# Feed-forward stages with eight pairs instead of six, each followed by half of a four-chunk down product

## The chip, the cores and the metric

The kernel runs on one core of one Trainium2 chip. The metric is the device time of one execution in microseconds (us). Engines are named as the profile names them: PE (TensorE, matmul), DVE (VectorE), ACT (ScalarE), POOL (GpSimd), SP (SyncE, which issues the DMAs).

## The reference, cut to what matters

512 positions of width 1024 go through two blocks. Each has mixers that this change leaves alone, and there are three gated feed-forward stages: one in the first block, two in the second.

```python
def rms_norm(x, g, eps=NORM_EPS):
    x32 = x.astype(jnp.float32)
    y = x32 * lax.rsqrt(jnp.mean(x32 * x32, axis=-1, keepdims=True) + eps)
    return (y * g.astype(jnp.float32)).astype(x.dtype)

# first block, D_FF = 2816
h = rms_norm(x, norm_ffn_pre_g[l])
f = (jax.nn.silu(h @ w_gate[l]) * (h @ w_up[l])) @ w_down[l]
x = x + rms_norm(f, norm_ffn_post_g[l])

# second block, twice
def swiglu(h, w_gu, w_down):
    gu = h @ w_gu
    gate, up = jnp.split(gu, 2, axis=-1)
    return (jax.nn.silu(gate) * up) @ w_down
x = x + 0.5 * swiglu(rmsnorm(x, ffn1_norm[l]), ffn1_w_gu[l], ffn1_w_down[l])
```

All is float32.

## The kernel before

**Storage.** Activations lie transposed: 128 features on the partitions, 512 positions along the free axis, so a width of 1024 is 8 chunks. Each float32 operand is split in two rounded parts, high (`HH`, `GH`, `WH`) and low (`HL`, `GL`, `WL`), and every product is three matmuls: high by high, low weight by high, high weight by low (lines 1328, 1330, 1332). An output tile of 128 features from 8 chunks is 24 matmuls of 512 columns; one from 4 chunks is 12.

**Weights.** Each weight tile is loaded whole by SP into one of four slots `RAW` (line 2432). ACT then makes the high part (`split`, line 1573) and DVE the low part (line 1864). The parts live in a ring of six halves; a weight tile takes two halves whatever its number of chunks, a weight of a pair (below) takes one. ACT may write a half only when PE has finished the weight that held it, and SP may fill a raw slot only when DVE has made the low part of what lay there (`raw_done`).

**Pairs.** A feed-forward stage has 22 output tiles for the gate and 22 for up. Two tiles that stand side by side can be made together, as a *pair*: `pair` replaces 2x2x2 block products of half size by seven (`MIXED`, Winograd's form). One side of a pair (gate or up) is 7 products of 4 chunks x 3 matmuls = 84 matmuls of 256 columns (`product`, lines 1356, 1358, 1360), where two plain tiles are 48 of 512. Four of the seven weights are sums of weight blocks, which POOL makes from two raw slots (`combine_weights`, line 2311, sums 1 to 4). The products are added up by DVE (lines 1890, 1900, 1903, 1908, 1917, 1926), ACT applies silu, and POOL multiplies gate by up for three quarters of the pair (`gate_mixed`, line 2333: one of 128x512, one of 128x256; the "gate products"). Then `split_tile` (ACT line 1667, DVE line 1982) writes the two tiles of the pair into `GH` and `GL`, where the down product reads them. The seventh product adds onto a bank that DVE's line 1903 must have read.

**A stage** (`ffn`, called once per stage) works in thirds, `THIRDS`: 6, 8 and 8 tiles. The first six tiles are plain (`PLAIN`), since the mixed inputs are only being made then. In each other third, pairs stand at tiles 0, 3 and 6 (`PAIRS`) and a plain tile at 2 and 5. After each third the down product over that third's 6 or 8 chunks follows, 8 output tiles `mt`, and DVE adds each to `X` or to the stage's output tiles (lines 2098, 2080, 2083). During the first down product, `place` (ACT line 1583, DVE line 1883) writes the normalized input over `HH` and `HL`, one chunk per output tile. The last third of the last stage is done by `last_down`, whose last 4 chunks run in two halves of positions.

**Order.** There is no scheduler on the chip. A `Plan` lists steps; each engine runs its own steps strictly in that order and waits by semaphores. `ahead` and `split_to` put the split of a weight where its ring halves are certain to come free. `split_to` also puts the sums of a coming pair: after each split it looks at the next 8 weights (`LOOK`) and emits sums whose raws have been asked for, as long as fewer than 2 whole (not pair) weights stand in between.

## Time and profile before

| | us |
|---|---|
| runs | 1922.88, 1921.64, 1922.81 |
| median | 1922.81 |
| the profiled execution | 1921.05 |
| its span | 1919.3 |

The span is what the profile's rows cover; 1.75 us lie around it. The profile's page gives busy times by engine and by fortieths of the span, and the trace gives every instruction with its start, its duration and the idle time ahead of it. A matmul's duration overlaps the next one's, so what one costs is read from the distance between starts. Busy shares: PE 99%, DVE 64%, ACT 44%, POOL 26%.

### The profile page before, as it was taken

How to read it: one execution, taken by the hardware profiler on the slowest of the kernel's cores; microseconds unless marked ns; L12 is line 12 of the kernel's file. 1: busy time of each engine (PE TensorE's matmuls, PEld its weight loads, DVE VectorE, ACT ScalarE, POOL GpSimd, SP SyncE). 2: the span in 40 equal slices, each digit the busy share in tenths (PEclk: the TensorE clock that was granted, in tenths of full speed). 3: DMA queues.
4: the chain of work that ended last, by engine and by line, in shares of the span. 5: the costliest groups of instructions: out<-in, count | busy, mean ns of one | idle time of the engine just before them, and what ended most of it. 6: DMA issues, size and time to landing. Idle time of an engine off the chain costs nothing.

```text
span 1919.3 us, 27787 instructions
## 1 busy us (share of the span) xinstructions
PE 1895.8 (99%) x10930; PEld 1602.8 (84%) x10930; DVE 1231.6 (64%) x1869; ACT 852.3 (44%) x1453; POOL 498.7 (26%) x422
## 2 busy tenths in 40 slices
PE   9999999999999999999999999999899999999998
PEld 7777788878998998789989888777777788998997
DVE  6677535476775674767657657887754456775665
ACT  6344524454443443544424446665543344442444
POOL 5101001214352431225323432222010023442330
PEclk9999999999999999999999999999999999999999
DMA  6222133332433343333434332222332233333332
GB/s 175 60 66 67 55 105 101 114 99 83 116 89 110 88 120 100 88 88 88 114 87 119 100 99 67 67 67 67 88 99 57 76 88 91 108 89 110 89 104 83
DMA packets 340787, 176.56 MB, mean 92 GB/s; under 512 B 6481, under 2 KB 339378, under 8 KB 340658
## 3 DMA queue, kind: packets, MB, share of 16 engines
q1 hardware_dynamic: 340658, 174.79, 31.6%
q8 instruction: 87, 1.43, 0.3%
q14 instruction: 42, 0.34, 0.1%
HBM read 172.67 MB, written 2.10 MB: 91 GB/s over the span
## 4 chain that ended last, share of the span: by engine, by line
PE 84%; DVE 7%; issue 3%; ACT 3%; POOL 2%; DMA 1%; ACTq 0%; SPq 0%; POOLq 0%; DVEq 0%
PE ps L1328 21%; PE ps L1332 20%; PE ps L1330 20%; PE ps L1356 5%; PE ps L1360 5%; PE ps L1358 5%; DVE WL L1864 2%; PE ps L1422 1%; POOL TS L2311 1%; DMA RAW<-in_ffn_w_gu 1%; POOL TS L2333 1%; DVE GL L1982 1%; PE ps L1402 1%; PE ps L1411 1%; PE ps L1507 1%
## 5 line engine op out<-in xcount | busy, mean ns | idle before, releaser
L1864 DVE TENSOR_TENSOR WL<-RAW,WH 128x1024 fp32r<-128x1024 f32 (+2 forms) x371 | 408.6, 1107 | 221.1 <-ACT WH L1573 217.7
L1573 ACT ACTIVATE WH<-RAW 128x1024 fp32r<-128x1024 f32 (+2 forms) x371 | 326.2, 886 | 312.7 <-PE ps L1332 264.6
L1328 PE MATMUL ps<-HH,WH 128*128 128x512 f32 x1152 | 461.4, 400 | 1.0 <-ACT HH L1620 1.0
L1332 PE MATMUL ps<-HL,WH 128*128 128x512 f32 x1152 | 449.7, 390 | 0.8 <-DVE HL L1946 0.8
L1330 PE MATMUL ps<-HH,WL 128*128 128x512 f32 x1152 | 449.1, 390 | 0.4 <-DVE WL L1864 0.4
L1328 PE MATMUL ps<-GH,WH 128*128 128x512 f32 x688 | 269.4, 392 | 0.0
L1332 PE MATMUL ps<-GL,WH 128*128 128x512 f32 x688 | 268.1, 390 | 0.0
L1330 PE MATMUL ps<-GH,WL 128*128 128x512 f32 x688 | 267.9, 389 | 0.0
L1328 PEld LDWEIGHTS ps<-HH,WH 128*128 128x128 f32 x1152 | 216.3, 188 | 53.5 <-issue 8.2
L1332 PEld LDWEIGHTS ps<-HL,WH 128*128 128x128 f32 x1152 | 216.2, 188 | 49.1 <-DVE HL L1946 2.1
L1330 PEld LDWEIGHTS ps<-HH,WL 128*128 128x128 f32 x1152 | 216.5, 188 | 47.7 <-issue 4.1
L2311 POOL TENSOR_TENSOR TS<-RAW 128x512 f32<-128x512 f32 x72 | 102.3, 1421 | 352.4 <-issue 259.8
L1360 PE MATMUL ps<-NL,WH 128*128 128x256 f32 x576 | 163.0, 283 | 0.0
L1358 PE MATMUL ps<-NH,WL 128*128 128x256 f32 x576 | 163.0, 283 | 0.0
L1356 PE MATMUL ps<-NH,WH 128*128 128x256 f32 x576 | 162.9, 283 | 0.0
L1864 DVE TENSOR_TENSOR WL<-TS,WH 128x512 fp32r<-128x512 f32 x144 | 132.0, 927 | 42.0 <-ACT WH L1573 40.5
L1332 PEld LDWEIGHTS ps<-GL,WH 128*128 128x128 f32 x688 | 129.1, 188 | 28.1 <-DVE GL L1982 1.3
L1328 PEld LDWEIGHTS ps<-GH,WH 128*128 128x128 f32 x688 | 129.2, 188 | 27.8 <-ACT GH L1667 0.8
L1330 PEld LDWEIGHTS ps<-GH,WL 128*128 128x128 f32 x688 | 129.2, 188 | 27.0 <-issue 0.5
L2342 POOL TENSOR_TENSOR TS<-TS 128x512 f32<-128x512 f32 (+1 forms) x42 | 53.0, 1261 | 297.0 <-ACT TS L1631 294.6
L1356 PE MATMUL ps<-HH,WH 128*128 128x256 f32 x432 | 123.2, 285 | 3.0 <-DVE TS L1903 2.8
L1358 PE MATMUL ps<-HH,WL 128*128 128x256 f32 x432 | 122.2, 283 | 0.0
(251 smaller groups left out, 3048.6 us busy)
## 6 DMA issues: line engine op xcount, KB each, us to landing
RAW<-in_ffn_w_gu SPq DMA_DIRECT2D x88, 512.0 KB, 3.8
RAW<-in_w_in SPq DMA_DIRECT2D x67, 512.0 KB, 3.7
RAW<-in_ffn_w_down SPq DMA_DIRECT2D x24, 512.0 KB, 3.8
RAW<-in_w_gate SPq DMA_DIRECT2D x22, 512.0 KB, 3.9
RAW<-in_w_up SPq DMA_DIRECT2D x22, 512.0 KB, 3.8
RAW<-in_w_out SPq DMA_DIRECT2D x16, 512.0 KB, 3.7
RAW<-in_mem_w_kv SPq DMA_DIRECT2D x16, 512.0 KB, 3.8
RAW<-in_w_down SPq DMA_DIRECT2D x16, 512.0 KB, 3.8
```

The lines of the kernel that those rows point to most:

```text
L1328: e.matmul(bk, wh, xh, start=k == 0, stop=False)
L1330: e.matmul(bk, wl, xh, start=False, stop=False)
L1332: last = e.matmul(bk, wh, xl, start=False, stop=k == kt - 1)
L1356: e.matmul(bk, wh[:, c, :], xh, start=i < 5 and c == 0, stop=False, skip_group_check=i >= 5)
L1358: e.matmul(bk, wl[:, c, :], xh, start=False, stop=False, skip_group_check=i >= 5)
L1360: o = e.matmul(bk, wh[:, c, :], xl, start=False, stop=c == 3, skip_group_check=i >= 5)
L1402: e.matmul(at.bank(("sc", (u, half), i))[:, 0:n], at.tile(q[0])[s, i * P:(i + 1) * P], at.tile(k[0])[s, 0:n], start=True, stop=True).then_ ...
L1411: o = e.transpose(bk[:, c:c + P], m["L"][half][:, lo[i] + j * P:lo[i] + (j + 1) * P], ident)
L1573: e.activation(at.weight(n, "H"), at.raw(n), ACT.Copy).then_inc(*sg.inc("hi", n))
L1864: e.tensor_tensor(at.weight(n, "L"), at.raw(n), at.weight(n, "H").bitcast(F32), ALU.subtract).then_inc(*sg.inc("lo", n))
L2311: e.tensor_tensor(out, x, y, op).then_inc(*sg.inc("comb", (key, j)))
L2342: e.tensor_tensor(a, a, s, ALU.add).then_inc(*sg.inc("acc", (acc, c)))
```

## The change

`THIRDS` and `PAIRS` go. A stage now has six plain tiles, then `SEGMENTS`: pieces of the down product over 4 chunks (`"down", n, first chunk, chunks, first mt, last mt`) and pairs by turns. Eight pairs cover tiles 6 to 21. Each four-chunk down product is cut in two halves, one ahead of a pair and one behind it: 5 and 3 output tiles for the first, 4 and 4 for the other three. What remains, `REST`, is the down product over chunks 16 to 21, after the last pair. So each output tile is added up in five parts and not three. `place` handles two chunks per output tile in the first four. The split tiles of a pair are emitted behind the second and third output tile of the down piece that follows. `last_down` keeps its 4 chunks in halves of positions and has 2 chunks ahead of them in place of 4. `split_to` emits sums while fewer than 3 whole weights stand in between.

```diff
-THIRDS = ((0, 6), (6, 8), (14, 8))
-PAIRS = ((), (0, 3, 6), (0, 3, 6))
+SEGMENTS = (("down", 0, 0, 4, 0, 5), ("pair", 6), ("down", 0, 0, 4, 5, KD), ("pair", 8),
+            ("down", 1, 4, 4, 0, 4), ("pair", 10), ("down", 1, 4, 4, 4, KD), ("pair", 12),
+            ("down", 2, 8, 4, 0, 4), ("pair", 14), ("down", 2, 8, 4, 4, KD), ("pair", 16),
+            ("down", 3, 12, 4, 0, 4), ("pair", 18), ("down", 3, 12, 4, 4, KD), ("pair", 20))
+REST = (16, 6)
+LAST = 4
...
-                if w[0] == "sum" and need < self.n_dma and whole < 2:
+                if w[0] == "sum" and need < self.n_dma and whole < 3:
                     self.combine_to(w[1], max(w[2], self.combined.get(w[1], 0)))
...
+        for kind, n, *rest in SEGMENTS:
+            if kind == "pair":
+                G, f = third0 + n // 8, n % 8
+                self.pair(gen, G, f, 0, gate, g0 + n * P, pending)
+                done = self.pair(gen, G, f, 1, up, u0 + n * P, pending)
...
+            for mt in range(m0, m1):
+                b = self.bank(("db", third0, f0, mt))
+                if n == 0 and mt < 4:
+                    self.place(gen, next(unplaced), plain)
+                    self.place(gen, next(unplaced), plain)
+                mm, = self.mtiles([(down, f0, nf, mt * P)], ("G", third0 + f0 // 8, f0 % 8), [b], ahead=False)
+                evac(n, mt, b, mm)
+                if mt > m0 and pending:
+                    self.split_tile(*pending.pop(0))
+                self.ahead(len(self.weights))
...
+        for first, cnt in GROUPS:
+            mts = range(first, first + cnt)
+            banks = [self.bank(("db", third0, f0, mt)) for mt in mts]
+            mms = self.mtiles([(down, f0, nf, mt * P) for mt in mts], ("G", third0 + f0 // 8, f0 % 8), banks, ahead=False)
...
-            mm, = self.mtiles([(down, f0, nf - 4, mt * P)], ("G", G, 0), [b])
+            mm, = self.mtiles([(down, f0, 2, mt * P)], ("G", G, 0), [b])
```

**POOL around the end of a pair.** L2311 are the sums for the next pair, L2333 the gate products of the pair that ends; the semaphores `s_d_raw` tell that a raw slot has landed. Before, with a plain tile between the pairs:

```order
104 L2311 TENSOR_TENSOR TS<-RAW 128x512 [waits s_xl,s_d_raw3,s_d_raw2]
105 L2311 TENSOR_TENSOR TS<-TS,RAW 128x512 [waits s_lo,s_comb]
106 L2311 TENSOR_TENSOR TS<-RAW 128x512 [waits s_lo]
107 L2311 TENSOR_TENSOR TS<-RAW,TS 128x512 [waits s_lo,s_comb]
108 L2333 TENSOR_TENSOR TS<-TS 128x512 [waits s_gate_act,s_part_sum]
109 L2311 TENSOR_TENSOR TS<-RAW 128x512 [waits s_lo,s_d_raw1,s_d_raw0]
110 L2311 TENSOR_TENSOR TS<-TS,RAW 128x512 [waits s_lo,s_comb]
111 L2333 TENSOR_TENSOR TS<-TS 128x256 [waits s_gate_act,s_part_sum]
```

After, with four down tiles between the pairs:

```order
94 L2333 TENSOR_TENSOR TS<-TS 128x512 [waits s_gate_act,s_part_sum]
95 L2311 TENSOR_TENSOR TS<-RAW 128x512 [waits s_xl,s_d_raw1,s_d_raw0]
96 L2311 TENSOR_TENSOR TS<-TS,RAW 128x512 [waits s_lo,s_comb]
97 L2311 TENSOR_TENSOR TS<-RAW 128x512 [waits s_lo]
98 L2333 TENSOR_TENSOR TS<-TS 128x256 [waits s_gate_act,s_part_sum]
99 L2311 TENSOR_TENSOR TS<-RAW,TS 128x512 [waits s_comb]
100 L2311 TENSOR_TENSOR TS<-RAW 128x512 [waits s_lo,s_d_raw3,s_d_raw2]
101 L2311 TENSOR_TENSOR TS<-TS,RAW 128x512 [waits s_lo,s_comb]
```

The second gate product stands behind the first three sums of the next pair, as it stood behind six sums before.

**DVE between two pairs.** L1917 and L1926 are a pair's last additions, L1864 the low parts of weights (from `TS`: of a sum; from `RAW`: of a whole tile or a half), L1982 the split tiles, L2073 the plain tile's product, L2083 the addition of a down tile. Before:

```order
568 L1917 TENSOR_TENSOR TS<-ps,TS 128x256 [waits s_mm]
569 L1864 TENSOR_TENSOR WL<-TS,WH 128x512 [waits s_hi]
570 L1926 TENSOR_TENSOR TS<-ps,TS 128x256 [waits s_mm]
571 L1864 TENSOR_TENSOR WL<-TS,WH 128x512 [waits s_hi]
572 L1864 TENSOR_TENSOR WL<-RAW,WH 128x512 [waits s_hi]
573 L1864 TENSOR_TENSOR WL<-TS,WH 128x512 [waits s_hi]
574 L1982 TENSOR_TENSOR GL<-TS,GH 128x512 [waits s_part_sum,s_gm,s_xh]
575 L1982 TENSOR_TENSOR GL<-TS,GH 128x512 [waits s_xh]
576 L1864 TENSOR_TENSOR WL<-RAW,WH 128x512 [waits s_hi] x2
577 L2073 TENSOR_TENSOR TS<-ps,TS 128x512 [waits s_gate_act,s_mm]
```

After:

```order
591 L2083 TENSOR_TENSOR TS<-ps,TS 128x512 [waits s_dn,s_mm]
592 L1864 TENSOR_TENSOR WL<-RAW,WH 128x512 [waits s_hi]
593 L2083 TENSOR_TENSOR TS<-ps,TS 128x512 [waits s_dn,s_mm]
594 L1982 TENSOR_TENSOR GL<-TS,GH 128x512 [waits s_part_sum,s_gm,s_xh]
595 L1864 TENSOR_TENSOR WL<-TS,WH 128x512 [waits s_hi] x2
596 L2083 TENSOR_TENSOR TS<-ps,TS 128x512 [waits s_dn,s_mm]
597 L1982 TENSOR_TENSOR GL<-TS,GH 128x512 [waits s_xh]
598 L1864 TENSOR_TENSOR WL<-RAW,WH 128x512 [waits s_hi]
599 L1864 TENSOR_TENSOR WL<-TS,WH 128x512 [waits s_hi]
600 L2083 TENSOR_TENSOR TS<-ps,TS 128x512 [waits s_dn,s_mm]
601 L1864 TENSOR_TENSOR WL<-RAW,WH 128x512 [waits s_hi] x2
```

Before, the first four weights of the next pair (569 to 573) stood ahead of the first split tile; after, the first two (595) stand behind it.

## Rows read from the trace of the kernel before

**Rows 1.** The page: busy time of PE, and its busy and clock slices.

```profile
PE 1895.8 (99%) x10930; PEld 1602.8 (84%) x10930; DVE 1231.6 (64%) x1869; ACT 852.3 (44%) x1453; POOL 498.7 (26%) x422
...
PE   9999999999999999999999999999899999999998
...
PEclk9999999999999999999999999999999999999999
```

**Rows 2.** Windows of stage one (stretch, length, busy by engine, clock, DMA): pair, plain tile, down.

```profile
504.73:524.88 20.15, 20.15 (x169) 20.15 (x168) 14.43 (x24) 9.76 (x17) 3.38 (x3) 1.00 0.46 130
524.88:535.79 10.91, 10.91 (x51) 9.02 (x49) 6.08 (x7) 3.57 (x7) 10.83 (x9) 1.00 0.17 50
...
713.81:757.35 43.54, 43.54 (x194) 36.04 (x193) 19.12 (x20) 13.29 (x17) 8.49 (x7) 1.00 0.34 99
```

**Rows 3.** Timeline of PE (start, duration in us): first matmul of a pair, plain tile, next pair.

```profile
504.73 0.28 PE L1356 MATMUL ps<-NH,WH 128*128 128x256 f32 x1
...
524.88 0.40 PE L1328 MATMUL ps<-HH,WH 128*128 128x512 f32 x1
...
535.79 0.28 PE L1356 MATMUL ps<-NH,WH 128*128 128x256 f32 x1
```

**Rows 4.** PE's waits in pairs: groups by form (busy, mean ns, idle before), and timeline.

```profile
L1356 PE MATMUL ps<-HH,WH 128*128 128x256 f32 x432 | 123.2, 285 | 3.0 <-DVE TS L1903 2.8
...
576.11 0.39 PE L1356 MATMUL ps<-HH,WH 128*128 128x256 f32 x1 [0.47 <-DVE TS L1903]
```

**Rows 5.** SP: timeline of raw loads in the first pair, and the page's time to landing.

```profile
515.32 2.40 SPq L2432 DMA_DIRECT2D RAW<-in_w_gate  x2
...
RAW<-in_w_gate SPq DMA_DIRECT2D x22, 512.0 KB, 3.9
```

**Rows 6.** Timeline of POOL: first pair's end, plain tile; after the third pair.

```profile
522.15 1.30 POOL L2311 TENSOR_TENSOR TS<-RAW 128x512 f32<-128x512 f32 x1 [16.69 <-DVE WL L1864]
523.53 2.22 POOL L2311 TENSOR_TENSOR TS<-TS,RAW 128x512 f32<-128x512 f32 x1
525.71 1.29 POOL L2311 TENSOR_TENSOR TS<-RAW 128x512 f32<-128x512 f32 x1
526.96 1.74 POOL L2311 TENSOR_TENSOR TS<-RAW,TS 128x512 f32<-128x512 f32 x1
528.66 1.73 POOL L2333 TENSOR_TENSOR TS<-TS 128x512 f32<-128x512 f32 x1
...
533.31 1.18 POOL L2333 TENSOR_TENSOR TS<-TS 128x256 f32<-128x256 f32 x1
...
589.07 0.74 POOL L2333 TENSOR_TENSOR TS<-TS 128x256 f32<-128x256 f32 x1 [1.83 <-DVE TS L1926]
```

**Rows 7.** Timeline of DVE in the same stretch.

```profile
526.44 1.10 DVE L1864 TENSOR_TENSOR WL<-TS,WH 128x512 fp32r<-128x512 f32 x1 [1.51 <-ACT WH L1573]
...
527.80 1.45 DVE L1864 TENSOR_TENSOR WL<-TS,WH 128x512 fp32r<-128x512 f32 x1
531.27 0.93 DVE L1864 TENSOR_TENSOR WL<-RAW,WH 128x512 fp32r<-128x512 f32 x1 [2.02 <-ACT WH L1573]
...
535.19 2.81 DVE L1982 TENSOR_TENSOR GL<-TS,GH 128x512 fp32r<-128x512 f32 x2 [1.29 <-ACT GH L1667]
```

**Rows 8.** Groups by form: ACT's high part of a half; DVE's low part of it.

```profile
L1573 ACT ACTIVATE WH<-RAW 128x512 fp32r<-128x512 f32 x132 | 80.5, 623 | 110.8 <-PE ps L1332 102.5 <-PE ps L1360 7.9
...
L1864 DVE TENSOR_TENSOR WL<-RAW,WH 128x512 fp32r<-128x512 f32 x132 | 97.5, 749 | 59.2 <-ACT WH L1573 57.0
```

**Rows 9.** Timeline of DVE in the first down product of stage one: L1883 place, L2080 addition.

```profile
475.65 0.68 DVE L1883 TENSOR_TENSOR HL<-TS,HH 128x512 fp32r<-128x512 f32 x1
...
490.42 1.78 DVE L1883 TENSOR_TENSOR HL<-TS,HH 128x512 fp32r<-128x512 f32 x1
492.69 0.69 DVE L2080 COPY TS<-ps 128x512 f32<-128x512 f32 x1 [0.48 <-PE ps L1332]
```

**Rows 10.** Timeline of DVE in the last stage's last product, where POOL is idle.

```profile
1876.70 0.69 DVE L1864 TENSOR_TENSOR WL<-RAW,WH 128x512 fp32r<-128x512 f32 x1 [1.43 <-ACT WH L1573]
```

More of the change, by code:

```diff
@@ new lines, in ffn, with before @@
+        R, pending, unplaced = None, [], iter(range(KD))
+        for f in range(PLAIN):
+            key = (third0, f)
+            bg, bu = self.bank(("gb", key)), self.bank(("ub", key))
+            sg, su = (gate, 0, KD, g0 + f * P), (up, 0, KD, u0 + f * P)
+            if f == 0 and gen in SUMMED:
+                sums = iter(range(-1, KD))
+                def before():
+                    c = next(sums)
+                    if c >= 0:
+                        self.sum_square(("n", gen), c)
+                mg, mu = self.mtiles([sg, su], ("H", gen, 0), [bg, bu], before=before)
+                before()
+            elif f == 0:
+                mg, mu = self.mtiles([sg, su], ("H", gen, 0), [bg, bu])
+            else:
+                mg, = self.mtiles([sg], ("H", gen, 0), [bg])
+            t, go = self.normed(gen, ("gt", key), bg, mg, 1.0, "Silu")
+            R = self.norm(gen)
+            self.step("gate_r", key, go, R)
+            if f:
+                self.mix_split(gen, f - 1)
+            if f == PLAIN - 1:
+                self.tiles.give(("R", ("n", gen)), ("N", (gen, 7)), ("gr", key))
+            if f:
+                mu, = self.mtiles([su], ("H", gen, 0), [bu])
+            self.step("gate_up", key, mu, bu, ("gr", key))
+            self.banks.give(bu, ("gu", key))
+            self.split_tile(("gt", key), ("gu", key), "G", third0, f)
+            self.tiles.give(("gt", key), ("xl", ("G", third0, f)))
+            if f < PLAIN - 1:
+                self.mix(gen, f, gcol)
@@ new lines, in ffn @@
+        plain = mu
+        for kind, n, *rest in SEGMENTS:
[3 more added lines that the diff above has]
+                done = self.pair(gen, G, f, 1, up, u0 + n * P, pending)
+                for a in range(2):
+                    pending.append((("gt", (G, f + a)), ("gm", ((G, f, 1), a)), "G", G, f + a, (("part_sum", ("c11", (G, f, 1))),)))
+                continue
+            f0, nf, m0, m1 = rest
+            for mt in range(m0, m1):
[4 more added lines that the diff above has]
+                mm, = self.mtiles([(down, f0, nf, mt * P)], ("G", third0 + f0 // 8, f0 % 8), [b], ahead=False)
+                evac(n, mt, b, mm)
+                if mt > m0 and pending:
+                    self.split_tile(*pending.pop(0))
+                self.ahead(len(self.weights))
+            self.gfree = (mm,)
@@ new lines, in ffn @@
+        while pending:
+            self.split_tile(*pending.pop(0))
+        self.hfree = self.mixed_free = (done,)
+        for half in range(2):
+            self.held["L", half] = self.held["PT", half] = (done,)
+        f0, nf = REST
+        if gen == 5:
+            self.last_down(down, f0, nf, third0 + f0 // 8, evac)
+            return
+        for first, cnt in GROUPS:
+            mts = range(first, first + cnt)
+            banks = [self.bank(("db", third0, f0, mt)) for mt in mts]
+            mms = self.mtiles([(down, f0, nf, mt * P) for mt in mts], ("G", third0 + f0 // 8, f0 % 8), banks, ahead=False)
+            for mt, b, mm in zip(mts, banks, mms):
+                evac(LAST, mt, b, mm)
+                if gen == 2:
@@ L602, in ffn @@
                     for i in LATE[mt]:
                         self.step("consts", i, done)
-                self.ahead(len(self.weights))
-            self.gfree = (mm,)
+            self.ahead(len(self.weights))
+        self.gfree = (mm,)
     def post_norm(self, gen, outs, acc, acc_ev, gcol, nextcol, heads):
@@ L877, in evac @@
             self.banks.give(b, ev)
-            if third == 2:
+            if third == LAST:
                 outs.append((key, ev))
@@ L1102, in last_down @@
                 if h == 0:
-                    self.weigh((down, f0 + nf - 4, 4, mt * P, mt))
-                self.groups.append((n + mt, 1, ("G", G, nf - 4), [b], slice(256 * h, 256 * h + 256), 4))
-                for k in range(4):
+                    self.weigh((down, f0 + 2, nf - 2, mt * P, mt))
+                self.groups.append((n + mt, 1, ("G", G, 2), [b], slice(256 * h, 256 * h + 256), nf - 2))
+                for k in range(nf - 2):
                     self.step("mm", len(self.groups) - 1, k)
```

80 lines of the change are left out of this document (4 added, 76 removed).

## The prediction

> **What bounds the kernel now.** I read the page first: PE is busy 99% of the span, every slice of it is at 8 or 9 tenths, and the granted clock is 0.9 or more throughout, the higher of the two levels, 2.4 GHz [rows 1]. So the time is PE's own work, and any other engine matters only where it makes PE wait. Then I read windows of the first feed-forward stage: a pair takes 20.15 us with PE busy all of it, a plain tile (gate and up) 10.91, a down product over 8 chunks 43.54, without a gap [rows 2]. The starts in the timeline give the pace [rows 3]: a pair has 168 matmuls of 256 columns in 20.15 us, 0.120 us each; a plain tile 48 of 512 columns in 10.91 us, 0.227 each. PE's only waits in pairs are on DVE's line 1903, ahead of the seventh product, 3.0 us in all [rows 4].
>
> **Part one: PE's work.** Each stage turns four plain tiles into two pairs. Per stage that takes away 4 x 48 = 192 matmuls of 512 columns (43.6 us) and adds 336 of 256 (40.3 us), so 3.3 us go; in three stages 576 x 0.2273 - 1008 x 0.1199 = 130.9 - 120.9 = **-10.0 us**. The matmuls of the down product keep their number and size: they are only cut in other groups.
>
> The Trainium skill (TensorE: Matmul & The Clock Gate, section Back-to-back issue gap) gives N/2.4 + 2.5 ns between matmuls in isolation. By it the exchange would save 576 x 0.2158 - 1008 x 0.1092 = 14.2 us. The rows have 0.227 and 0.120, both about 11 ns longer, and the measurement decides; the sum by the rule would be 4.2 us lower.
>
> **Part two: what hides behind PE, and what it costs on average.** Sixteen more down tiles per stage are added up by DVE, 0.69 us each [rows 9], and in the whole kernel 64 splits of 8 chunks and 8 of 6 give way to 172 of 4 chunks and 8 of 2. In the new rhythm, pair and four down tiles, 31.06 us of PE, DVE does what it did in a pair (14.43 and, with the split tiles, up to 18), and 4 x (0.75 + 0.69) = 5.8 us for the down tiles [rows 2, 8, 9]: some 24 of 31. On average that fits. It is the order that counts, so I follow one transition.
>
> **Part three: the transition from a pair to the next, 18 of them with four down tiles between.** T is the moment at which PE ends the pair and starts the first down tile. Four tiles of 12 x 0.227 = 2.72 us each: the next pair is due at T+10.9.
>
> The raws. The next pair's gate side needs two raw slots. The second one is the slot of the second down tile, free when DVE has that tile's low part. Its ring halves come free after up's fifth product, at T-2.9; PE's tail of 0.2, ACT 0.62 [rows 8], DVE 0.69 [rows 10] make T-1.3. A load lands 3.9 us later [rows 5]: **T+2.6**. Before, the corresponding load was issued at about 517.4, 7.5 us ahead of the pair's end at 524.88 [rows 3, 5], and the sums began at 522.15, 2.7 us ahead of it [rows 6]. So the sums start 5.3 us later than they did, with the same time left to the next pair.
>
> POOL. Three sums took from 522.15 to 526.96, 4.8 us [rows 6]. They end at T+7.4. Behind them in POOL's order waits the pair's last gate product, 1.18 us [rows 6]: T+8.6. That wait is the change's own: with the old bound of 2 whole weights the sums would be emitted behind this gate product, whose inputs are ready at about T+1.
>
> ACT and DVE. The pair's first split tile needs that gate product and stands ahead of the next pair's first weights on both engines. ACT 0.62: T+9.2. DVE: while POOL works, DVE's operations on two SBUF operands take 1.10, 1.45, 0.93 and 2.81/2 = 1.4 [rows 7], where they take 0.69 with POOL idle [rows 10]. POOL has the fourth sum and up's sums to make until about T+16. So the split tile ends at T+10.6, the first weight's low part at T+12.0 where PE's second matmul wants it at T+11.0: PE waits **1.0**. Then on DVE the second weight (T+13.4), a down addition 0.69 (T+14.1), the other split tile 1.4 (T+15.5), the third weight 0.93 (T+16.4); PE wants it at T+10.9+1.0+2.9+0.1 = T+14.9: **1.5** more. After that POOL is idle, DVE takes 0.69 for each weight and PE 1.44, and DVE is in time again, but for line 1903, which may be late by 0.3 as at 576.11 [rows 4]. I take 2.5 us per transition, **18 x 2.5 = +45 us**. From below: with 0.74 for the gate product, its shorter row [rows 6], and DVE not slowed for the split tiles, the third weight is still late by some 0.6. From above: with 1.78 for each slowed operation, as a place shows [rows 9], 3.5.
>
> The rule behind the slowed rows is in the Trainium skill (SBUF — State Buffer, section SBUF: two separate sides): DVE with two SBUF inputs and GpSimd share one port pair, whoever starts first holds it for its whole instruction, and "the other fully blocks". The 1.10 to 1.78 against 0.69 agree. Taken strictly, each DVE operation would wait out a sum of 1.3 to 1.75 us, which gives the upper 3.5 per transition and not 2.5, 18 us more.
>
> **Part four: the three places with three down tiles (pair 6 to 8).** PE is back at T+8.2. Only the first down tile's slot is in the way there, so the raws land at T-0.3, but three sums, both gate products and the fourth sum stand in a row on POOL: -0.3 + 4.8 + 1.7 + 1.7 + 1.2 = T+9.1 [rows 6]. The split tile passes DVE at T+11.1, the third weight at T+12.0 against T+11.2 wanted, the fifth, behind the second split tile, some 1.2 us late. I take 2 us, bounds 1 and 3: **+6 us**.
>
> **Part five: the start of a stage, three times.** In the first down product DVE had one place of 0.68 (1.78 with POOL at work) per 4.1 us. Now it is two per 2.72 us. In the first 13.6 us it has 8 places, 5 additions, 3 splits, and the last plain tile's two operations: 8 x 0.68 + 5 x 0.69 + 3 x 0.75 + 1.4 = 12.5 us if nothing is slowed, 8.8 more if all places are [rows 9]. POOL makes the sums of pair 6 from about 5.5 us on, when their raws land, so about half is slowed: 17 us against 13.6. I take 4 us, bounds 1 and 7: **+12 us**.
>
> **Part six: ends.** The remaining down product has 6 chunks, 4.1 us a tile, with additions and feeds behind; the last stage has eight tiles of 1.36 us on PE against 0.69 for the addition and some 0.4 for the split on DVE, an estimate from half of the 0.69 of a split twice as long [rows 10]. Bounds 0 and 4, **+1.5**. What goes: the 3.0 us of waits in today's third pairs [rows 4], which I counted anew above: **-3**.
>
> **The sum.** -10.0 - 3 + 45 + 6 + 12 + 1.5 = +51.5. The profiled execution took 1921.05, so it would take 1972.6; the median of the runs lies 1.8 above it: **1974**. With all bounds low: -13 + 10.8 + 3 + 3 = +4, 1927. With all high: -13 + 63 + 9 + 21 + 4 = +84, 2007.
>
> **Rivals.**
> - *Nothing waits, faster.* The mechanism: the gate product is out of the way early. It decides at about T+5: if the pair's last gate product ends before that, the split tile passes DVE before the next weights come, and PE has its weights by T+10.9. It would need the sums to start before T-1, as at 522.15 [rows 6]. Then 1922.8 - 10.0 - 3 = 1910. For it: DVE and POOL have the time on average. Against it: the slot of the second down tile. Chance 0.12.
> - *Only the start of a stage is late.* The transitions just hold (0.3 each or less), places cost 12, the short pieces 4: 1922.8 - 13 + 16 + 4 = 1930. Chance 0.10, and 0.04 beside it for waits so few that the time comes out within 0.2%.
> - *DVE doesn't recover.* The lateness lasts into up's side, 4 us or more per transition: 1922.8 - 13 + 75 + 20 = 2005. Chance 0.08. Against it: POOL is idle in the pair's middle, 3.38 us in 20.15 [rows 2].
> - *The change doesn't do what it says.* By the order listings it does: the pairs are there, and so are the sums ahead of the gate product.
>
> **Numbers.** Main case 0.66, with 1935 to 2000 as its own range. A difference of 0.2%, 3.8 us, is what a measurement of this kernel can tell from none. Faster by more: 0.12; within: 0.04; slower by more: 0.84. The range that leaves out the faster rival and the far end: 1925 to 2000.
>
> **What would show it.** PE's groups: 1152 - 192 matmuls of 512 columns from `HH`, 432 + 144 and 576 + 192 of 256. Idle time of PE ended by line 1864 (low parts) in the first and third product of a pair, 1 to 1.5 us each, and by line 1903 in the seventh; POOL's 128x256 gate product ending 8 to 9 us after the pair; ACT's line 1667 waiting for it; the first sum starting 2.6 us after the pair's end, released by a DMA. The pair-to-pair distance would be 33.5 us, not 31.06. I am wrong if that distance is 31.1, or if the gate product ends within 5 us of the pair.

## The result and the profile after

| | before | after |
|---|---|---|
| median of the runs, us | 1922.22 (4 runs, 1921.51 to 1922.88) | 1995.47 (4 runs, 1994.15 to 1997.04) |
| ratio to before | | 1.038, interval 1.036 to 1.040 |
| span of the profiled execution | 1919.3 | 1993.7 |

The change costs 73.3 us. 1974 was forecast, in a range of 1925 to 2000: slower, inside the range, by a sum that was 21.5 us short.

The first lines of the page (busy time by engine, and slices) are set against [rows 1]. PE's share falls from 99 to 96%. Its busy time is 12.5 us longer, although by the pace of its starts it has 10 us less to do: the modelled ends of matmuls cover part of the gaps around a wait. The slices of the clock stay at 9.

```profile
PE 1908.3 (96%) x11362; PEld 1621.0 (81%) x11362; DVE 1363.4 (68%) x2079; ACT 888.3 (45%) x1579; POOL 574.8 (29%) x482
...
PE   9999999999989899999898999999999999999998
...
PEclk9999999999999999999999999999999999999999
```

PE's waits over the whole of the kernel after (total, times, longest). Before there was nothing on the first line; the third answers to [rows 4].

```profile
PE ps L1358 <- DVE WL L1864: 60.8, 47, 2.5
...
PE ps L1356 <- DVE TS L1903: 2.6, 6, 0.5
```

47 waits for 24 pairs, about two in each. The groups by form: the products that read `NH` (the first of a side is one) and those that read `HH` (the third is one).

```profile
L1358 PE MATMUL ps<-NH,WL 128*128 128x256 f32 x768 | 222.6, 290 | 21.2 <-DVE WL L1864 21.1
...
L1358 PE MATMUL ps<-HH,WL 128*128 128x256 f32 x576 | 165.7, 288 | 39.7 <-DVE WL L1864 39.7
```

One transition from a pair over four down tiles to the next pair, in stage one of the kernel after. T, the end of the pair, is 576.24. First PE's timeline (start, duration, idle before): the first down tile, the next pair's first matmul, and its two late low parts.

```profile
576.24 0.40 PE L1328 MATMUL ps<-GH,WH 128*128 128x512 f32 x1
...
587.14 0.28 PE L1356 MATMUL ps<-NH,WH 128*128 128x256 f32 x1
588.36 0.38 PE L1358 MATMUL ps<-NH,WL 128*128 128x256 f32 x1 [0.94 <-DVE WL L1864]
...
593.43 0.39 PE L1358 MATMUL ps<-HH,WL 128*128 128x256 f32 x1 [1.68 <-DVE WL L1864]
```

SP's timeline: the two loads of the next gate side. The row ends with the second one's issue, at 572.33 + 3.97 = 576.30, so that load is issued at about T.

```profile
572.33 3.97 SPq L2432 DMA_DIRECT2D RAW<-in_w_gate  x2
```

POOL's timeline. Before, the same sums began 2.7 us ahead of the pair's end [rows 6]. Now they begin 3.6 us behind it, and the 128x256 gate product of line 2333 comes after three of them.

```profile
574.06 1.29 POOL L2333 TENSOR_TENSOR TS<-TS 128x512 f32<-128x512 f32 x1 [15.69 <-DVE TS L1908]
579.88 1.28 POOL L2311 TENSOR_TENSOR TS<-RAW 128x512 f32<-128x512 f32 x1 [4.52 <-issue]
581.23 1.63 POOL L2311 TENSOR_TENSOR TS<-TS,RAW 128x512 f32<-128x512 f32 x1
582.82 1.28 POOL L2311 TENSOR_TENSOR TS<-RAW 128x512 f32<-128x512 f32 x1
584.06 0.74 POOL L2333 TENSOR_TENSOR TS<-TS 128x256 f32<-128x256 f32 x1
```

ACT's timeline: it stands idle for the gate product, with the next pair's weights queued behind.

```profile
584.83 0.63 ACT L1667 ACTIVATE GH<-TS 128x512 fp32r<-128x512 f32 x1 [4.96 <-POOL TS L2333]
```

DVE's timeline: the low part that frees the raw slot (574.30), the split tile (585.50), the first two weights of the next pair, the second split tile, the third weight (591.63). [rows 7] are their like before.

```profile
574.30 1.60 DVE L1864 TENSOR_TENSOR WL<-RAW,WH 128x512 fp32r<-128x512 f32 x1 [0.32 <-ACT WH L1573]
...
585.50 1.11 DVE L1982 TENSOR_TENSOR GL<-TS,GH 128x512 fp32r<-128x512 f32 x1 [2.90 <-ACT GH L1667]
586.53 3.47 DVE L1864 TENSOR_TENSOR WL<-TS,WH 128x512 fp32r<-128x512 f32 x2
...
590.53 1.18 DVE L1982 TENSOR_TENSOR GL<-TS,GH 128x512 fp32r<-128x512 f32 x1
591.63 1.75 DVE L1864 TENSOR_TENSOR WL<-RAW,WH 128x512 fp32r<-128x512 f32 x1
```

DVE is idle from 582.59 to 585.50, just ahead of the operations that PE then waits for. Here it isn't short of time: what it needs comes late.

**A measure for all kernels.** The waits that the profile names leave out small delays. So I took, over all matmuls of all pairs, the distance between starts beyond the usual 0.120 us: what *pairs lose*. Before it is 5.2 us, after 85.6. For the transition above it is 3.41: 1.10 at the first product (588.36 instead of 587.26), 1.84 at the third, small ones between.

### The profile page after: what moved, and what is told of

The parts are those of the page before. It is cut to its first block, busy times and chain, and to the rows that moved or that the text cites. A ratio compares the mean times of both kernels' runs of the same rounds, so it can differ in the third digit from the quotient of the medians.

```text
span 1993.7 us, 29397 instructions
## 1 busy us (share of the span) xinstructions
PE 1908.3 (96%) x11362; PEld 1621.0 (81%) x11362; DVE 1363.4 (68%) x2079; ACT 888.3 (45%) x1579; POOL 574.8 (29%) x482
## 4 chain that ended last, share of the span: by engine, by line
PE 71%; DVE 16%; issue 4%; DMA 4%; ACT 4%; POOL 1%; SPq 0%; ACTq 0%; DVEq 0%; POOLq 0%
PE ps L1328 15%; PE ps L1330 15%; PE ps L1332 15%; DVE WL L1864 7%; PE ps L1358 7%; PE ps L1360 6%; PE ps L1356 6%; DVE GL L1982 2%; DMA RAW<-in_ffn_w_gu 2%; DVE HL L1883 1%; ACT WH L1573 1%; PE ps L1422 1%; DMA RAW<-in_w_up 1%; DVE X L2098 1%; PE ps L1402 1%
## 5 line engine op out<-in xcount | busy, mean ns | idle before, releaser
L1864 DVE TENSOR_TENSOR WL<-RAW,WH 128x512 fp32r<-128x512 f32 (+3 forms) x431 | 446.6, 1043 | 192.6 <-ACT WH L1573 187.1
L1573 ACT ACTIVATE WH<-RAW 128x512 fp32r<-128x512 f32 (+3 forms) x431 | 331.8, 777 | 251.0 <-PE ps L1332 127.1
L1328 PE MATMUL ps<-HH,WH 128*128 128x512 f32 x960 | 386.8, 403 | 0.6 <-ACT HH L1620 0.4
L1332 PE MATMUL ps<-HL,WH 128*128 128x512 f32 x960 | 374.8, 390 | 0.8 <-DVE HL L1946 0.8
L1330 PE MATMUL ps<-HH,WL 128*128 128x512 f32 x960 | 374.6, 390 | 0.7 <-DVE WL L1864 0.7
L1358 PE MATMUL ps<-NH,WL 128*128 128x256 f32 x768 | 222.6, 290 | 21.2 <-DVE WL L1864 21.1
L1356 PE MATMUL ps<-NH,WH 128*128 128x256 f32 x768 | 217.7, 283 | 0.3 <-ACT WH L1573 0.3
L1360 PE MATMUL ps<-NL,WH 128*128 128x256 f32 x768 | 217.6, 283 | 0.0
L1864 DVE TENSOR_TENSOR WL<-TS,WH 128x512 fp32r<-128x512 f32 x192 | 177.6, 944 | 30.6 <-ACT WH L1573 30.6
L2311 POOL TENSOR_TENSOR TS<-RAW 128x512 f32<-128x512 f32 x96 | 146.8, 1529 | 160.2 <-issue 148.8
L1358 PEld LDWEIGHTS ps<-NH,WL 128*128 128x128 f32 x768 | 147.4, 192 | 33.0 <-DVE WL L1864 32.9
L1360 PE MATMUL ps<-HL,WH 128*128 128x256 f32 x576 | 163.2, 283 | 0.0
```

What stands on the lines that cost most here:

```text
L1328: e.matmul(bk, wh, xh, start=k == 0, stop=False)
L1330: e.matmul(bk, wl, xh, start=False, stop=False)
L1332: last = e.matmul(bk, wh, xl, start=False, stop=k == kt - 1)
L1356: e.matmul(bk, wh[:, c, :], xh, start=i < 5 and c == 0, stop=False, skip_group_check=i >= 5)
L1358: e.matmul(bk, wl[:, c, :], xh, start=False, stop=False, skip_group_check=i >= 5)
L1360: o = e.matmul(bk, wh[:, c, :], xl, start=False, stop=c == 3, skip_group_check=i >= 5)
```

## The experiments

Two theories about the wait were to be told apart, and one about what it would take to be rid of it.
- *The knot*: the new look-ahead puts the sums ahead of the pair's last gate product on POOL. The sums wait for a raw, so the gate product does too, and with it ACT, DVE and the next weights.
- *The raw*: a four-chunk down weight occupies a whole raw slot, so the pair's raws are late, whatever the order.
- *Capacity*: eight pairs are too much for DVE and POOL, whatever the order and the buffers.

### The look-ahead alone

In the kernel after, the bound goes back to two:

```diff
-                if w[0] == "sum" and need < self.n_dma and whole < 3:
+                if w[0] == "sum" and need < self.n_dma and whole < 2:
```

> The changed kernel with one number put back: sums are emitted while fewer than 2 whole weights stand in between, as before the change. On POOL the last gate product of a pair then stands ahead of the next pair's sums wherever four down tiles stand between the pairs. Theory A (PE waits because the split tile waits for a gate product that stands behind sums whose raws land late): the 128x256 gate product ends within 2 us of the pair's end, and of the 3.0 to 4.5 us of PE waits per pair at the 18 places with four down tiles at most 0.5 are left; the 3 places with three down tiles and the 3 first pairs keep theirs. Time 1995.5 - 18 x 3 = 1941, between 1930 and 1950. Theory B (DVE and POOL slow each other at the same operands, whatever the order): the same work meets in the same 10.9 us, so at least 2 us per pair stay; time 1975 to 1995.

Measured: 1957.35 us, ratio 1.0185 (1.017 to 1.020); pairs lose 48.8. The time lies between the ranges of the two theories, nearer to A. So the look-ahead, which was part of the change, costs 38.1 of its 73 us. More is left in the pairs than the 0.5 us each that A allowed. In the first pair of each stage it is 4.8 to 5.3, in the others about 1.5 (2.6 in one). The waits of this kernel have moved:

```profile
PE ps L1358 <- DVE WL L1864: 12.2, 12, 2.5
PE ps L1356 <- DVE TS L1903: 10.9, 21, 0.5
```

In this kernel the pair ends at 573.48 and the first sum starts at 577.19, 3.7 us later, with no gate product in the row of eight sums behind it. The knot is gone and the late raw is not.

The same bound of three in the kernel before:

> The kernel before with the bound at 3 whole weights instead of 2 and nothing else. Theory A: in this order the raws of the next pair land 2.7 us ahead of the end of the pair, so sums that stand ahead of a gate product hold it up by little; pairs wait as before, 5 us in all, time within 2 us of before. If the bound of 3 costs by itself, whatever the rhythm of pairs and down tiles, the time rises by 10 us or more.

Measured: 1921.75 us, ratio 0.9999 (0.999 to 1.0009). That equality shows less than it seems. The edit puts the sums earlier in the plan, but not past any other step of POOL: POOL's order of operations in the two traces is the same. So this run is no test of the look-ahead. What it could have shown stands in the kernel before as it is: its gate product of 128x256 is behind six sums, which begin ahead of the pair's end [rows 6], and all its pairs together lose 5.2 us. The run with five slots, below, shows the same for the kernel after.

### The knot cut in another way

The look-ahead stays at three, but DVE makes the 128x256 gate product, so that it can't stand behind sums (the lines shown are DVE's; POOL's `gate_mixed` leaves that product out):

```diff
+    def gate_mixed(key, a):
+        if a:
+            return
...
+        e.tensor_tensor(t, t, w, ALU.mult).then_inc(*sg.inc("gq", (key, a)))
```

> The changed kernel, bound of 3 and the late raws kept, but the 128x256 gate product is made by DVE instead of POOL, right behind the pair's last addition. Theory A: the split tile no longer waits for POOL's three sums; it passes DVE by T+7.5 (T is the pair's end), PE's wait in the next pair's first product goes, the one in the third falls below 1 us, so some 2.5 us go at each of 18 places and some at the 3 shorter ones: 1945, between 1935 and 1960. Theory B: POOL's sums still overlap DVE's weights from T+3.6 on and DVE has more work, so the time stays above 1980.

Measured: 1959.94 us, ratio 1.0197 (1.018 to 1.021); pairs lose 50.9. It is at the upper end of theory A's range, and it is the result of the bound of two within 2.6 us, with the look-ahead untouched. So the knot is what the look-ahead does, 36 to 38 us by either cut, and the residue of about 1.5 us for each pair is common to both.

### The order on DVE

The loads, the sums and the late gate product stay; only the split tiles are queued behind the next weights' splits:

```diff
                 evac(n, mt, b, mm)
+                self.ahead(len(self.weights))
                 if mt > m0 and pending:
                     self.split_tile(*pending.pop(0))
-                self.ahead(len(self.weights))
```

> The changed kernel with one order changed: in the four-tile down pieces the split tiles of the last pair (ACT's L1667 and VectorE's L1982) stand behind the splits of the next pair's weights instead of ahead of them. Loads, sums and the late gate product stay as they are. With T the end of a pair: the raws land at T+2.6 or a little later, the first two sums end at T+6, the first weight's low part at T+8, while the gate product ends at T+8.6 and its split tile now passes at about T+11, when the first two weights have been split. Theory A (the price of the change is paid because the split tile holds the weights back behind the gate product): pair losses fall from 85.6 to 15 to 35 us, the whole to 1930 to 1950 us. Theory B (the late landing and GpSimd's doubled operations are enough by themselves; the order on VectorE hardly matters): 1975 to 1995 us.

Measured: 1975.48 us, ratio 1.0275 (1.026 to 1.029); pairs lose 65.2. That is the lower edge of theory B's range, and far from A's: 20 us of the 80 are back, not 50 or more. It isn't nothing either. DVE's timeline, with the pair's end at 575.57 and the next pair due at 586.48:

```profile
582.79 2.25 DVE L1864 TENSOR_TENSOR WL<-TS,WH 128x512 fp32r<-128x512 f32 x2 [0.86 <-ACT WH L1573]
585.19 1.55 DVE L1982 TENSOR_TENSOR GL<-TS,GH 128x512 fp32r<-128x512 f32 x1
586.66 0.68 DVE L2083 TENSOR_TENSOR TS<-ps,TS 128x512 f32<-128x512 f32 x1
587.27 1.18 DVE L1864 TENSOR_TENSOR WL<-RAW,WH 128x512 fp32r<-128x512 f32 x1
588.37 1.78 DVE L1864 TENSOR_TENSOR WL<-TS,WH 128x512 fp32r<-128x512 f32 x1
590.07 1.77 DVE L1982 TENSOR_TENSOR GL<-TS,GH 128x512 fp32r<-128x512 f32 x1
...
592.37 1.77 DVE L1864 TENSOR_TENSOR WL<-RAW,WH 128x512 fp32r<-128x512 f32 x2
```

The first four weights are in time, and the waits in the first and third product are gone. The fifth weight (592.37) now has both split tiles ahead of it, and PE waits 1.2 us for it in the fifth product, at 593.59, and 0.7 us at the seventh, for line 1903. The work that the late gate product has piled up must be done somewhere.

### Five raw slots

In the kernel after; two scratch tiles are given up for the room:

```diff
-NRAW = 4
+NRAW = 5
 NSPL = 3
-NTILE = 23
+NTILE = 21
```

> The changed kernel with five raw slots instead of four, and 21 tiles of scratch instead of 23 to make room. The second raw of the next pair's gate side then needs the slot of the first down tile and not of the second, so it is asked for about 3 us earlier. Theory A: the three sums start at about the pair's end and not 3.6 us behind it, the gate product ends near 5 us behind it, the first weight of the next pair is in time, and 1 us or less of waits per pair is left at the 18 places: time 1995.5 - 18 x 2.5 = 1950, between 1940 and 1962. Theory B: POOL works as long as it did in the same stretch, waits stay above 2 us per pair, time above 1980.

Measured: 1935.76 us, ratio 1.0072 (1.0057 to 1.0087); pairs lose 23.6. That is 60 us back, more than the 45 expected, with the look-ahead of three still there. POOL's timeline in this kernel, around a pair that ends at 667.46: the sums start 0.1 us ahead of that, and the gate product behind them is out of the way at 672.73, 5.3 us behind it, not 8.6.

```profile
667.35 1.29 POOL L2311 TENSOR_TENSOR TS<-RAW 128x512 f32<-128x512 f32 x1 [0.77 <-issue]
...
671.55 1.18 POOL L2333 TENSOR_TENSOR TS<-TS 128x256 f32<-128x256 f32 x1
```

This pair's successor loses 0.14 us. So the knot costs next to nothing where the raw is in time: both are one chain, and the raw stands at its head.

Is the slot then a gain of its own, which the kernel before would have too? The same edit there:

> The kernel before with five buffers for landed weights and 21 scratch tiles. It shows what the buffer is worth without the change: its pairs lose 5.2 us in six places. Expected 1918 to 1923 us: if the buffer were worth much here too (below 1915 us), then five buffers would not be a cure for the change but a gain of their own.

Measured: 1918.97 us, ratio 0.9984 (0.9974 to 0.9993); pairs lose 2.5 instead of 5.2. Its wait at line 1903 falls to 0.7 us, from 2.8 [rows 4].

```profile
PE ps L1356 <- DVE TS L1903: 0.7, 3, 0.3
```

The slot is worth 3 us before and 60 after: it is a cure for what the change does. It is also, narrowly, the version that beats both kernels.

### Both cures

Five slots and the bound of two:

> The changed kernel with five buffers for weights that have landed instead of four (two scratch tiles fewer, 21 for 23, pay for it) and with the look-ahead of the sums back at two weights of a down product. Five buffers alone gave 1935.8 us, the bound of two alone 1957.4 us, the change 1995.5 us. Theory A (every pair waits for one chain: a buffer comes free late, so the last part of a weight lands late, so its three GpSimd sums, the gate product behind them and the VectorE split behind that are late; either edit takes the cause away and the two don't add): 1928 to 1938 us, pair losses at 15 to 25 us in all, three quarters of it in the first pair of each stage. Theory B (the two edits hit different waits and add, 38 and 60 us off): below 1915 us.

Measured: 1948.27 us, ratio 1.0138 (1.012 to 1.016); pairs lose 37.4. Neither theory: the bound of two, worth 38 us with four slots, costs 12.5 with five. In this kernel a pair ends at 671.05. The first sum waits for no load, but it is now queued behind the gate product, and POOL stands idle until that has its input:

```profile
671.76 0.74 POOL L2333 TENSOR_TENSOR TS<-TS 128x256 f32<-128x256 f32 x1 [1.58 <-DVE TS L1926]
672.46 1.73 POOL L2311 TENSOR_TENSOR TS<-RAW 128x512 f32<-128x512 f32 x1
```

The eight sums then run without a gap to 685.33, beside all of DVE's work for the transition, and 21 pairs lose 1.1 us each, at the third product. With the raws in time the look-ahead of three is right, with the raws late it is wrong. I had priced the two orders by when inputs are ready, but had not seen that the sign depends on it.

### The start of a stage

With five slots most of what is left is in the first pairs: 2.5, 5.4 and 5.2 us. DVE's timeline in the second stage of the kernel with five slots: a place in twos (line 1883) is 3.45 us beside POOL's sums, which run here from 862.09 to 868.44, and 1.28 alone.

```profile
860.39 1.28 DVE L1883 TENSOR_TENSOR HL<-TS,HH 128x512 fp32r<-128x512 f32 x2
861.59 0.68 DVE L2098 SCALAR_TENSOR_TENSOR X<-ps,X 128x512 f32<-128x512 f32 x1
862.19 3.42 DVE L1864 TENSOR_TENSOR WL<-TS,WH 128x512 fp32r<-128x512 f32 x2
865.54 3.45 DVE L1883 TENSOR_TENSOR HL<-TS,HH 128x512 fp32r<-128x512 f32 x2
```

PE then waits 2.87 us at 870.24, and runs at a lower clock for some 4 us behind that (last section). So I spread the places: one beside each of the first five down tiles, three between products of the first pair. Once with five slots, once with this edit alone on the kernel after (the last two lines stand in `pair`, behind each product):

```diff
-                if n == 0 and mt < 4:
-                    self.place(gen, next(unplaced), plain)
+                if n == 0 and mt < 5:
                     self.place(gen, next(unplaced), plain)
...
+            for c in late[i:i + 1]:
+                self.place(gen, *c)
```

> The changed kernel with five buffers for landed weights and 21 scratch tiles, bound of three as in the change, and the eight splits that place the normed input (ACT copy, VectorE difference) put one beside each of the first five down tiles of a stage and the last three between products of the first pair, instead of two beside each of the first four tiles. With five buffers and bunched splits the first pairs of the three stages lose 2.5, 5.4 and 5.2 us (13.1 together) and the whole is 1935.8 us. Theory A (the bunched splits put VectorE behind where GpSimd's sums double their time, and this makes the first pair late): first pairs lose under 2 us each, whole 1925 to 1931 us. Theory B (the first pair is late because its weights' last parts come late, whatever VectorE does): no change, 1934 to 1938 us.

Measured: 1932.64 us, ratio 1.0053 (1.0038 to 1.0068). First pairs lose 3.6 each, 10.8 together instead of 13.1; they were to lose under 2. The other pairs lose more, so all pairs lose 24.5 instead of 23.6. The medians still differ by 3.1 us and the profiled executions by 0.9, and what is gained isn't in the pairs: the matmuls of the down tiles (those that read `GH` or `GL`) start with 2.4 us less delay in all.

> The changed kernel with only the eight placing splits of a stage spread (one beside each of the first five down tiles, three between products of the first pair). In the changed kernel the first pairs lose 3.9, 4.4 and 5.1 us, the other pairs 3.4 each. If the late landing sets the floor of every pair and the bunched splits come on top: first pairs fall to 3.2 to 3.8 us, the whole from 1995.5 to 1991 to 1994 us. If the splits are the whole of what first pairs lose: 1982 to 1985 us.

Measured: 1994.68 us, ratio 1.038 (1.036 to 1.039), no different from the change; first pairs lose 5.6, 4.1 and 5.6 us. Theory A of the first run is wrong as a whole, and its time fits neither of its two ranges. The spread places arrive late themselves, which PE's waits in the kernel with five slots and spread places show (its lines stand one lower; 1884 is the place):

```profile
PE ps L1361 <- DVE HL L1884: 1.4, 3, 0.6
```

It looks as if the first pair of a stage has more DVE work around it than fits beside sums, so that an order only chooses who is late. No run takes work away there, so this isn't shown.

All three edits together, five slots, spread places, split tiles behind:

> The changed kernel with all three edits at once: five raw buffers with 21 scratch tiles, the placing splits spread, and the pair's split tiles behind the next pair's weights. Five buffers and spread splits alone gave 1932.6 us, with pair losses of 24.5 us (3.6 in each first pair, 1.5 in each second, 0.1 to 1.6 elsewhere). Theory A (what is left in the pairs past the first is still split tiles ahead of weights on VectorE): losses fall to 12 to 18 us, 1920 to 1927 us. Theory B (with the raws early the gate product is no longer late, so the order costs nothing): 1930 to 1935 us.

Measured: 1933.86 us, ratio 1.0062 (1.0047 to 1.0077); pairs lose 25.7. Theory B holds: with the raws early the order of the split tiles costs nothing.

### Eight pairs without the small fillers

The kernel before has a table for its pairs. Eight can be had by it, four in a row and then a whole down product of eight chunks; no down product is cut, the look-ahead is two.

```diff
-PAIRS = ((), (0, 3, 6), (0, 3, 6))
+PAIRS = ((), (0, 2, 4, 6), (0, 2, 4, 6))
```

> The kernel before with eight pairs a stage by its own table alone: PAIRS is ((), (0, 2, 4, 6), (0, 2, 4, 6)), so four pairs follow each other without a gap and a whole down product of eight chunks stands behind them. PE's work is that of the changed kernel (10.0 us less than before), four raw buffers, look-ahead bound of 2, down products not cut. Theory A (the change loses by its fillers: a four-chunk down weight takes a whole raw buffer and gives it back too late; pairs as such can be fed): few waits, 1910 to 1925 us. Theory B (eight pairs a stage are too much for GpSimd and VectorE wherever they stand, since a pair beside the next one has 20.2 us for eight sums of 1.3 to 1.75, two gate products and 14 to 18 us of VectorE): every pair behind a pair loses 1 us or more, 1930 us and above.

Measured: 1988.59 us, ratio 1.034 (1.032 to 1.036); pairs lose 80.2. Theory A is refuted: without the fillers it is as slow. And with five slots:

> Eight pairs a stage by the table of the kernel before, whole down products behind four pairs each, and five raw buffers with 21 scratch tiles. With four buffers it was 1988.6 us, with 80 us lost in pairs, 12.6 to 15.8 in each row of four. Its trace shows the same knot as the change: 515.67 to 529.77 three sums stand ahead of a gate product on GpSimd, and an in_w_gate load is issued only when the up side has begun. Theory A (the missing buffer is the cause there too): losses fall below 25 us, 1912 to 1933 us. Theory B (rows of pairs are too dense for VectorE and GpSimd, buffers or not): above 1950 us.

Measured: 1959.91 us, ratio 1.0197 (1.018 to 1.021); pairs lose 53.1. The missing slot is 27 of the 80 us here, not nearly all. More than half of the rest is one long wait in each row of four, behind its first pair: 4.7 to 5.3 us by starts, 28.9 in the six rows, and a lower clock behind it (last section). DVE's timeline in the first row, in the kernel with five slots (the second pair is at its gate side's seventh product):

```profile
532.88 1.11 DVE L1982 TENSOR_TENSOR GL<-TS,GH 128x512 fp32r<-128x512 f32 x1 [1.30 <-ACT GH L1667]
533.92 1.78 DVE L1864 TENSOR_TENSOR WL<-TS,WH 128x512 fp32r<-128x512 f32 x1
535.62 1.78 DVE L1982 TENSOR_TENSOR GL<-TS,GH 128x512 fp32r<-128x512 f32 x1
537.32 1.75 DVE L1864 TENSOR_TENSOR WL<-TS,WH 128x512 fp32r<-128x512 f32 x1
538.99 0.41 DVE L1890 TENSOR_TENSOR TS<-ps,TS 128x256 f32<-128x256 f32 x1
539.32 1.41 DVE L1864 TENSOR_TENSOR WL<-TS,WH 128x512 fp32r<-128x512 f32 x1
...
541.10 0.42 DVE L1903 TENSOR_TENSOR TS<-ps,TS 128x256 f32<-128x256 f32 x1
```

Five operations of two SBUF operands take 7.8 us beside POOL's sums; at 0.69 each, as alone, they would take 3.5. With them the additions at 1890 and 1903 come late, and PE, in the same kernel:

```profile
541.58 0.39 PE L1356 MATMUL ps<-HH,WH 128*128 128x256 f32 x1 [4.56 <-DVE TS L1903]
```

So capacity may have something to it, over a stretch of ten microseconds: a pair right behind a pair has nothing to hide the transition. No run takes work away from DVE or POOL, so it is argued from these rows. The fillers of the change hide most of it once the raws are there in time: with five slots 1936 us, against 1960 in rows.

### The runs side by side

The losses are from the one profiled execution of each kernel, so the difference is taken from that execution's time and not from the median, which is up to 2.2 us longer.

| kernel | median, us | profiled execution, us | pairs lose, us | difference |
|---|---|---|---|---|
| before (profiled with the change) | 1922.2 | 1921.05 | 5.2 | 1915.8 |
| before, bound of three | 1921.8 | 1922.99 | 5.4 | 1917.6 |
| before, five slots | 1919.0 | 1918.22 | 2.5 | 1915.7 |
| after | 1995.5 | 1995.40 | 85.6 | 1909.8 |
| after, bound of two | 1957.4 | 1956.25 | 48.8 | 1907.4 |
| after, gate product on DVE | 1959.9 | 1959.96 | 50.9 | 1909.1 |
| after, split tiles behind | 1975.5 | 1973.73 | 65.2 | 1908.5 |
| after, spread places | 1994.7 | 1993.65 | 86.2 | 1907.4 |
| after, five slots | 1935.8 | 1933.53 | 23.6 | 1909.9 |
| after, five slots, bound of two | 1948.3 | 1946.62 | 37.4 | 1909.2 |
| after, five slots, spread places | 1932.6 | 1932.64 | 24.5 | 1908.1 |
| after, all three edits | 1933.9 | 1932.66 | 25.7 | 1907.0 |
| eight in rows | 1988.6 | 1987.51 | 80.2 | 1907.3 |
| eight in rows, five slots | 1959.9 | 1959.92 | 53.1 | 1906.8 |

Without what its pairs lose, every kernel with eight pairs lies between 1906.8 and 1909.9 us, and those with six between 1915.7 and 1917.6, where the kernel before and its bound of three, the same work in the same order, are 1.8 us apart. So what lies outside these losses fell by some 8 us in the mean, and all but some 3 us of the differences among the kernels with eight pairs are what PE waits for in pairs.

## Why the prediction was right, and where its sum was short

**Part one, PE's work: right.** -10.0 was forecast from 0.2273 and 0.1199 us per start. The table has some -8 in the mean, -6 for the kernel after, and outside the pairs the distances between its starts are some 4 us longer than before, about 2 of them in the down tiles. The new matmuls of 256 columns start 0.12 us apart as the old ones did. The Trainium skill (TensorE: Matmul & The Clock Gate, section Back-to-back issue gap) gives its formula for a matmul in isolation, and the 14.2 us by it aren't borne out in this stream, where every matmul has a weight load of its own.

**Part three, the transition: mechanism right, price too low.** Every step stands in the rows: the sums behind the pair's end, the gate product behind three sums, ACT waiting for it, the split tile ahead of the weights, waits in the first and third product. It was put at 2.5 us, 45 for the 18; measured are 3.5 on average, 62.7 together, 3.0 to 3.7 in most and 4.5 in two. In those two, one of the next pair's loads took 5.4 and 5.7 us to land instead of 3.8, so the first sum started at T+5.2 and T+5.5; SP had issued the first of them at T-0.3, T being 610.69, as in the transition above, and no row says why it landed late:

```profile
610.38 0.37 SPq L2432 DMA_DIRECT2D RAW<-in_w_gate  x1
```

This term alone is 17.7 of the 21.5 us by which the sum was short. Its parts:
- The raw was to land at T+2.6 and the first sum starts at T+3.6. The low part that frees the slot was priced at 0.69; it met the 128x512 gate product (574.06) and took 1.60.
- Three sums take 4.2, not 4.8, and the gate product 0.74, not 1.18. So the gate product ends at T+8.6, as forecast, by errors that cancel.
- First wait 1.10, forecast 1.0. Third product 1.84, forecast 1.5; beside them 0.5 us of delays of 0.1 to 0.2 each that were not in the sum.
- Of the five slowed operations, the three low parts took 5.2 us (3.47 for two at 586.53, 1.75 at 591.63) and not 1.4 + 1.4 + 0.93 = 3.7; the two split tiles took 2.3 (585.50, 590.53) and not 2.8. So the lateness is 1.0 us more, most of it from the third weight, priced by the one row of 0.93 [rows 7].
- The upper bound of 3.5 was worked out wrongly. With 1.78 for all five, the steps as written bring the third weight at T+18.8, where PE wants it at T+13.9 if it hasn't waited: 4.9 us. The 3.5 measured isn't a case of every operation at the highest price. The rule that stands beside the bound, in the Trainium skill (SBUF — State Buffer, section SBUF: two separate sides), is that whichever of the two engines starts first blocks the other for its whole instruction. Beside POOL's operations nothing here took longer than 1.8 us, which is less than a sum of 1.28 and an own time of 0.69 put end to end. So the rule, taken as strictly as the prediction put it, would be too dear for these rows, and the mean of 1.4 was too cheap.

**Part four, three-tile places:** 3.0 to 3.4 us, forecast 2 (bounds 1 and 3); 3.5 us more in all. The first sum starts at T+0.4 in stage one and the gate product ends at T+8.7, where T-0.3 and T+9.1 were forecast. The next pair then loses 1.1 us at the third product, 0.8 at the fifth and 0.7 at the seventh, and the last of these wasn't in the forecast.

**Part five, the start of a stage:** 3.9, 4.4 and 5.1 us, forecast 4; 13.4 against 12. The size was right, its reason only partly: 1.5 us or so of the 5.1 in the last stage is a lower clock behind a wait of 2.54 us (last section), which wasn't in the sum. Spreading the places brings nothing in the kernel after; with five slots it brings 3.1 us by the medians, but not in the pairs.

**Part six, ends:** all matmuls that read `GH` or `GL` at 512 columns lose 5.9 us instead of 4.2, +1.7 against +1.5. Of the waits before I took off 3.0, by the profile's row; by starts they are 5.2.

**The rivals.** *Nothing waits* gave 1910 and named its condition: sums that start before T-1. The kernel with five slots comes near (T-0.1), and its pairs with four tiles lose 0.1 to 1.4. So the condition points the right way, and in the kernel after it wasn't met. *DVE doesn't recover* didn't happen: up's side loses next to nothing after the change. It does happen in the rows of pairs.

**What would show it:** the distance between pairs is 34.3 us (552.81 to 587.14), forecast 33.5. The three statements on waits hold, but for line 1903, whose 2.6 us in six places are no more than before; it becomes late (0.5 in 21 pairs) only when the knot is cut.

## What to carry to other kernels

When an in-order queue is told to look further ahead, list what it is moved past, and when the moved operation's own input comes: with an early input the look-ahead is a gain, with a late one it holds up everything behind it, and the same line changed sign here with one buffer more. A small weight in a buffer of full size occupies the whole buffer; count slots over a cycle before cutting products into pieces. (That one slot more is the cure is shown; two small weights in one slot weren't tried.) Price an operation by the row that it will stand in after the change: the low part that was put at 0.93 us took 1.75.

## What the runs showed of the hardware

**The price beside GpSimd.** DVE operations of 512 columns that read two SBUF operands take 0.67 to 0.69 us alone, all but 3 of 401 in the kernel after. Of the 121 there that begin and end beside a sum or gate product of POOL, 71 took 1.6 to 1.8 us, 49 took 1.1 to 1.3 and one 0.69, 1.50 in the mean; in the kernel before the mean is 1.38 over 75. Those that read PSUM keep their time (0.41 at 538.99, 0.68 at 586.66 above), sums or not. POOL's own vary too: in the kernel after a sum takes 1.3 to 1.8 us, and those that meet no such operation of DVE take 1.3, all 25; the small gate product takes 0.74 there, 1.18 with five slots. Before, the mean of the 128x512 low parts from `RAW` was 749 ns [rows 8]; after it is

```profile
L1864 DVE TENSOR_TENSOR WL<-RAW,WH 128x512 fp32r<-128x512 f32 x256 | 231.4, 911 | 63.8 <-ACT WH L1573 58.9
```

**A long wait can cost twice.** Behind the waits of an ordinary transition, 1 to 2 us, the granted clock stays 1.00 (in the 2.9 us behind a wait of 1.91, to 624.03, for one). Behind longer ones it may not. Windows (stretch, length, busy by engine, then the clock): in the kernel after, 2.9 us from the wait of 2.53 at the first pair of stage two, and 2.5 us from the wait of 2.54 at that of stage three; in the five-slot kernel with rows of pairs, the stretch before the wait of 4.56 us, behind it, and the next.

```profile
889.58:892.50 2.92, 2.92 (x22) 2.71 (x23) 2.92 (x4) 0.91 (x2) 1.09 (x1) 1.00 0.00 0
1689.98:1692.50 2.52, 2.52 (x14) 2.52 (x15) 2.52 (x3) 0.34 (x2) 1.08 (x1) 0.65 0.00 0
```

```profile
530.00:536.80 6.80, 6.80 (x59) 6.80 (x57) 5.50 (x5) 3.51 (x7) 6.53 (x5) 1.00 0.54 157
541.58:545.00 3.42, 3.42 (x17) 3.42 (x18) 2.11 (x4) 1.94 (x4) 0.00 (x0) 0.57 0.00 0
545.00:550.00 5.00, 5.00 (x42) 5.00 (x41) 2.90 (x6) 2.95 (x6) 0.90 (x1) 0.95 0.63 182
```

0.57 is a stretch mostly at the lower of the two levels, 1.2 GHz (0.50, as 3.4 us behind the long wait of the rows with four slots show throughout); matmuls of 256 columns then start 0.21 us apart instead of 0.12. In the kernel with rows and five slots some 17 of them do, about 1.5 us on top of the wait, until 545.6. The same follows the wait of 2.87 us with five slots (0.70 over the 2.8 us behind it). Between the two waits of the kernel after, 2.53 and 2.54 us, the clock stayed in one case and fell in the other. So what a wait of 2.5 us costs isn't settled by its length here.
